# The expert layer computed densely over all 16,384 experts, 256 tokens at a time, in place of gathering each token's 128 experts

## The chip, the cores and the metric

The kernel runs on one NeuronCore of a Trainium2 chip. The metric is the device time of one launch in microseconds (us), lower is better. All data are 32-bit floats.

## What is computed

One decoder layer for a prompt of 1024 tokens and for a sample group of 8 tokens, with D_MODEL = 1024. The layer projects the normalised input (1024 to 2816 columns), runs eight 64-wide heads of a recurrent delta-rule mixer beside a causal gated MLP in chunks of 128 tokens, projects back, then applies the expert layer (PEER), a gated per-layer embedding and a final norm. The part that the change rewrites is this:

```python
def peer_ffn(h, wq, subkeys, U, V):           # U, V: (16384, 1024)
    q  = (xt @ wq).reshape(T, 8, 2, 128)
    sc = einsum('thcd,cnd->thcn', q, subkeys)  # two scores of 128 keys for each of 8 heads
    sv, si = top_k(sc, 16)                     # 16 of 128, twice
    cand = sv[:, :, 0, :, None] + sv[:, :, 1, None, :]
    cv, ci = top_k(cand.reshape(T, 8, 256), 16)
    eidx = (si0 * 128 + si1)[ci]               # 8 x 16 = 128 experts of each token
    gate = softmax(cv)
    act  = gelu(einsum('tkd,td->tk', U[eidx], x)) * gate
    out  = einsum('tk,tkd->td', act, V[eidx])
```

So each token needs 128 rows of U and 128 rows of V out of 16,384. The outputs are the final rows of both groups, the new recurrent states, the shifted rows and the normalised rows of the sample group.

## The kernel before

The prompt is worked in NB = 8 blocks of 128 tokens, the partitions of a tile; the sample group is a ninth, narrow block. Three things run beside each other in iteration i, each engine (TensorE, VectorE, ScalarE, GpSimd, and SyncE for DMA) with its own program in an order written out by hand:

- the *front* of block i: norm, 11 weight chunks `win` (each 1024 x 256, two halves of 512 KB into the two buffers `wbuf`), shift, the mixer (`half(i, 0)` and `half(i, 1)`, four heads each), 4 chunks `wout`, norm, 8 query chunks `q`, top-16 searches (`top16`), the digit stages that turn candidate numbers into expert numbers, softmax;
- the *peer* work of block i-1: 128 steps. Step k of GpSimd gathers, by an indirect DMA, one U row and one V row for each of the 128 tokens (`uring`, `vring`, 8 slots each). VectorE multiplies the U rows with the tokens and sums (`expert`, L1611), ScalarE takes gelu of four at a time, VectorE weights them (`weigh`, L1592). The weighted sum of V rows is shared: of 128 steps 74 go to TensorE as a matmul with a diagonal matrix (ScalarE builds it, `diagonals`; `sum_v`, L979), the others to VectorE (L1604);
- the *tail* of block i-2: sum, norm, per-layer embedding (L957), 4 `gate` chunks, final norm, store.

`BOTH_STAGES` and `STAGE_WEIGHTS` spread the stages of front and tail over the 128 steps. `stream` (L755) is the matmul of a weight chunk: 8 matmuls of 128 x 128 weights by 256 columns, and after them TensorE waits for its own last result before it frees the buffer. Each 32-bit matmul stands as two records in the trace, so a chunk is 16 records; a transpose is one record. `load_w` issues a chunk's two DMAs from SyncE's queue when the buffer's last reader is done. Six PSUM banks rotate among the stages, two (`acc`) hold the expert sums.

Of the kernel before, what the change touches and what calls it, by code (L numbers as in the profile page):

```python
# [6 lines left out]
F32 = mybir.dt.float32  # L28
# [6 lines left out]
P = 128  # L35
# [15 lines left out]
NU, NV = 8, 8  # L51
NI = 4
UNIT = 4
UNITS = HK // UNIT
SPREAD = 123

PE_SHARE = {0: 2, 3: 1, 9: 3, 13: 2, 26: 4}
MOST_PE = max(PE_SHARE.values())
# [15 lines left out]
PER_BLOCK = {who: sum(len(who(n)) for n in range(UNITS)) for who in (pe_experts, ve_experts)}


def summed(who, i, n, j=UNIT - 1):

    if n < 0:
        i, n = i - 1, n + UNITS  # L80
    return (i - 1) * PER_BLOCK[who] + sum(len(who(m)) for m in range(n)) + sum(e <= j for e in who(n))

TAIL_STAGES = ["t_sum", "t_norm", "t_turn", "t_xT"] + [f"gate{c}" for c in range(5)] + ["y_norm", "y"]
NORM = lambda name: [f"{name}_{part}" for part in ("mean", "var", "root", "scale")]
HALF_STAGES = lambda g: (
    [f"h{g}_{part}" for part in ("turn", "products", "TT", "TI")]
    + [f"h{g}_{part}{m}" for m in range(1, LEVELS) for part in ("merge", "update")]
    + [f"h{g}_{part}" for part in ("solve", "SR0", "dS0", "SR1", "dS1", "Y")]  # L90
)
FRONT_STAGES = (
    ["norm", "turn", "xT"] + [f"win{c}" for c in range(11)] + ["shift0", "shift1", "shift2", "lora"] + NORM("ln") + ["lora_add", "kk", "gmlp", "key", "bonus", "kk_norm", "cum", "hats0", "hats1", "masked_v"]
    + [stage for both in zip(HALF_STAGES(0), HALF_STAGES(1)) for stage in both]
    + NORM("gn") + ["gn_bonus", "gn_gate"] + [f"wout{c}" for c in range(5)] + ["norm2", "xn2", "x2T"]
    + [stage for h in range(H + 2) for stage in [f"q{h}"] + ([f"ctop{h - 2}"] if h > 1 else []) + [f"top{h}"]] + ["soft"]
    + [f"digit{half}{part}" for half in range(2) for part in "abc"] + ["expert"]
)


HALF = lambda g: {
    3 * g: [f"aT{g}", f"rT{g}", f"MakT{g}"] + [f"TXt{g}{m}" for m in range(1, LEVELS)] + [f"SR{g}0", f"dS{g}1"],
    3 * g + 1: [f"bT{g}", f"MT{g}", f"MrbT{g}"] + [f"TX{g}{m}" for m in range(1, LEVELS - 1)] + [f"U1{g}", f"dS{g}0", f"Y{g}"],
    3 * g + 2: [f"kT{g}", f"M{g}", f"X{g}1", f"X{g}2", f"MrkT{g}", f"X{g}3", f"X{g}4", f"U0{g}", f"X{g}5", f"WT{g}", f"SR{g}1"],
}
SETUP_USES = {0: ["s_sk"], 1: ["s_ws0"], 2: ["s_ws1"], 3: ["s_vec"], 4: [], 5: []}
TAIL_USES = {
    0: ["t_xT0", "gate0", "gate2"], 1: ["t_xT1", "gate1", "gate3"], 2: ["ple0"], 3: ["ple1"], 4: ["t_pT"], 5: [],
}
_IN = {b: [f"xT{b}"] + [f"win{c}" for c in range(11) if c % 2 == b] for b in (0, 1)}  # L110
# [20 lines left out]
STAGE_WEIGHTS = {
    "t_sum": 33, "t_norm": 25, "t_turn": 15, "t_xT": 13, "gate4": 10, "gate": 48, "y_norm": 10, "y": 14, "norm": 12, "norm2": 12,
    "turn": 15, "xT": 14, "win": 55, "ln_mean": 26, "ln_var": 20, "ln_root": 5, "ln_scale": 30, "shift": 32, "lora": 55,
    "lora_add": 22, "kk": 34, "gmlp": 36, "key": 26, "bonus": 38, "kk_norm": 30, "cum": 18, "hats": 26, "masked_v": 28,
    "h_turn": 42, "h_products": 32, "h_TT": 38, "h_TI": 42, "h_merge": 48, "h_update": 18, "h_update5": 8, "h_solve": 28,
    "h_SR": 14, "h_dS": 14, "h_Y": 14, "gn_mean": 20, "gn_var": 16, "gn_root": 5, "gn_scale": 24, "gn_bonus": 18, "gn_gate": 20,
    "wout4": 8, "wout": 50, "xn2": 16, "x2T": 18, "q": 40, "top": 18, "q8": 22, "q9": 20, "top9": 1, "ctop": 24, "soft": 14,
    "digita": 48, "digitb": 46, "digitc": 38, "expert": 20,  # L140
}


# [1523 lines left out]
```

## Time and profile before

| | |
|---|---|
| median of 3 runs | 4841.38 us (4822.09 to 4863.28) |
| span of the profiled execution | 4840.4 us |
| TensorE busy (matmuls) | 3142.8 us, 65% |
| VectorE busy | 3066.2 us, 63% |
| GpSimd busy | 2461.0 us, 51% |
| ScalarE busy | 867.2 us, 18% |
| moved by DMA | 1407.59 MB, 291 GB/s |
| mean granted TensorE clock | 0.809 of full |

The profiled execution has no time of its own beside its span; the span differs from the median of the runs by 1 us, so a sum over the trace can stand for the time. Busy shares are means over the whole span: a front, the peer steps and a tail overlap in it.

### The profile page before, as it was taken

The page shows a single profiled execution, that of the slowest core. Times are in us where ns is not written, and L with a number is a line of the kernel's source. Part 1 is how long each engine was busy: PE and PEld are TensorE (multiplying, and loading weights), DVE is VectorE, ACT ScalarE, POOL GpSimd, SP SyncE. Part 2 cuts the span into 40 slices and gives each one's busy share as a digit, 9 for nine tenths or more (in the row PEclk, how much of TensorE's full clock was granted, in tenths as well). Part 3 has the DMA queues.
Part 4 walks back from the last instruction along what each step waited for, and adds up shares of the span by engine and source line. Part 5 has one row for each costly group of instructions (what it writes and reads, how often), then busy time and mean ns, then how long its engine had stood idle before and what let it go on. Part 6 is the DMA issues. An engine that isn't in the chain of part 4 may idle for free.

```text
span 4840.4 us, 48177 instructions
## 1 busy us (share of the span) xinstructions
PE 3142.8 (65%) x12962; PEld 2018.9 (42%) x12962; DVE 3066.2 (63%) x6057; ACT 867.2 (18%) x1858; POOL 2461.0 (51%) x2366
## 2 busy tenths in 40 slices
PE   4744676747766487747776396747777386764486
PEld 3643454425534265324544264334544255321152
DVE  1462968539584587639594586638685385857682
ACT  1110211202112211202112111202112121121112
POOL 1013765537455564537555474537655374557551
PEclk8777798869788698878888698878889697886668
DMA  4057899968989699968999699887989689999896
GB/s 144 30 153 263 292 349 330 331 230 313 320 310 359 215 350 342 320 239 313 316 320 368 209 324 332 307 290 269 357 303 342 225 318 319 317 358 312 311 318 214
DMA packets 648503, 1407.59 MB, mean 291 GB/s; under 512 B 44137, under 2 KB 369033, under 8 KB 648210
## 3 DMA queue, kind: packets, MB, share of 16 engines
q0 software_dynamic: 297216, 1082.26, 62.0%
q1 hardware_dynamic: 350994, 321.95, 20.7%
q8 instruction: 120, 1.97, 0.2%
q14 instruction: 173, 1.42, 0.1%
HBM read 1386.84 MB, written 9.93 MB: 289 GB/s over the span
## 4 chain that ended last, share of the span: by engine, by line
PE 33%; DVE 26%; DMA 22%; issue 10%; ACT 3%; SPq 3%; POOL 2%; DVEq 0%; POOLq 0%; ACTq 0%; PEldq 0%
PE peer_acc L979 11%; DMA wbuf<-in_w_in_dram 10%; PE bank L755 9%; DVE uring L1611 4%; DMA pa<-in_norm_ffn_g_dram 3%; DVE accv L1604 3%; DMA wbuf<-in_ple_gate_w_dram 3%; DMA proj_s<-pa 3%; DMA wbuf<-in_w_out_dram 2%; PE bank L843 2%; PE bank L893 2%; PE bank L877 1%; DVE feat L1443 1%; SPq L509 1%; PE bank L891 1%
## 5 line engine op out<-in xcount | busy, mean ns | idle before, releaser
L683 POOL DMA_INDIRECT vring<-in_peer_v_dram,idx_c x1024 | 1159.1, 1132 | 1278.2 <-PE peer_acc L979 858.0
L979 PE MATMUL peer_acc<-vring,dg 128*128 128x512 f32 x2368 | 1298.6, 692 | 456.7 <-ACT dg L1023 421.0
L673 POOL DMA_INDIRECT uring<-in_peer_u_dram,idx_c x1024 | 1160.8, 1134 | 660.1 <-issue 221.2
L1611 DVE CUSTOM_DVE_ANT_0 uring<-uring,px 128x1024 f32<-128x1024 f32 x1024 | 1243.7, 1223 | 94.0 <-DMA uring<-in_peer_u_dram,idx_c 66.6
L755 PE MATMUL bank<-wbuf,xT 128*128 128x256 f32 (+1 forms) x2736 | 760.2, 436 | 593.8 <-DMA wbuf<-in_w_in_dram 489.0
L979 PEld LDWEIGHTS peer_acc<-vring,dg 128*128 128x128 f32 x2368 | 486.3, 219 | 1055.3 <-issue 742.4
L755 PEld LDWEIGHTS bank<-wbuf,xT 128*128 128x128 f32 (+1 forms) x2736 | 549.9, 206 | 826.9 <-DMA wbuf<-in_w_in_dram 535.5
L1604 DVE SCALAR_TENSOR_TENSOR accv<-vring,pact,accv 128x1024 f32<-128x1024 f32 x424 | 544.5, 1284 | 15.7 <-issue 4.8
L1592 DVE TENSOR_TENSOR pact<-pg,pgate 128x4 f32<-128x4 f32 x256 | 40.4, 158 | 706.2 <-ACT pg L1023 705.7
L843 PEld LDWEIGHTS bank<-xT,wbuf 128*128 128x128 f32 x2304 | 307.4, 215 | 55.0 <-issue 49.0
L843 PE MATMUL bank<-xT,wbuf 128*128 128x128 f32 (+1 forms) x2304 | 306.3, 294 | 13.6 <-ACT xT L1023 7.3
L1023 ACT ACTIVATE dg<-ident,pact 128x128 f32<-128x128 f32 x592 | 200.3, 392 | 528.1 <-DVE pact L1592 524.1
L665 POOL COPY idx_c<-eidx 128x4 uint32 (+1 forms) x256 | 111.2, 435 | 342.7 <-DVEq L1222 327.3
L1023 ACT ACT_TABLE_LOAD x200 | 256.6, 1283 | 21.6 <-DMA z<-in_x_prompt_dram 15.8
L723 PE MATMUL bank<-ident,z 128*128 128x128 f32 (+1 forms) x288 | 53.1, 344 | 311.5 <-DVE z L1388 132.5
L1023 ACT ACTIVATE pg<-ph 128x4 f32<-128x4 f32 x257 | 52.3, 203 | 972.9 <-DVE ph L1611 955.2
L723 PEld LDWEIGHTS bank<-ident,z 128*128 128x128 f32 (+1 forms) x288 | 43.2, 185 | 335.7 <-issue 335.7
L1023 ACT ACTIVATE uv<-bank 128x256 f32<-128x256 f32 (+4 forms) x70 | 33.2, 484 | 632.0 <-PE bank L755 575.7
L1023 ACT ACTIVATE feat<-bank 128x256 f32<-128x256 f32 (+2 forms) x133 | 55.9, 421 | 268.5 <-PE bank L755 148.7
L1441 DVE MAX8 sv<-feat 128x8 f32<-128x128 f32 (+1 forms) x144 | 41.8, 290 | 95.4 <-ACT feat L1023 87.1
L1023 ACT ACTIVATE pa<-bank 128x256 f32<-128x256 f32 (+1 forms) x63 | 24.1, 383 | 435.3 <-PE bank L755 435.3
L1381 DVE TENSOR_TENSOR x<-bank,x 128x256 f32<-128x256 f32 (+1 forms) x36 | 15.2, 423 | 131.6 <-PE bank L755 101.6
(278 smaller groups left out, 3294.7 us busy)
## 6 DMA issues: line engine op xcount, KB each, us to landing
wbuf<-in_w_in_dram SPq DMA_DIRECT2D x198, 512.0 KB, 12.3
wbuf<-in_peer_wq_dram SPq DMA_DIRECT2D x144, 512.0 KB, 10.4
wbuf<-in_w_out_dram SPq DMA_DIRECT2D x72, 512.0 KB, 9.1
wbuf<-in_ple_gate_w_dram SPq DMA_DIRECT2D x72, 512.0 KB, 10.7
uring<-in_peer_u_dram,idx_c POOLq DMA_INDIRECT x1024, 6.5
vring<-in_peer_v_dram,idx_c POOLq DMA_INDIRECT x1024, 6.4
wbuf<-in_ple_w_dram SPq DMA_DIRECT2D x18, 512.0 KB, 6.8
feat<-in_shift_mu_dram SPq DMA_DIRECT2D x9, 896.0 KB, 11.6
```

What stands on the lines that cost most here:

```text
L509: sp.dma_start(at(i + 1), pa[P - 1:P, :]).then_inc(sig("proj_stored"), 16)
L665: gp.tensor_copy(idx_c[:, n % NI, :], src).then_inc(sig("idx_copied"), 1)
L673: gp.indirect_dma_start(uring[:, s, :], None, peer_u, bass.IndirectOffsetOnAxis(ap=idx_c[:, n % NI, j:j + 1], axis=0)).then_inc(sig(f"u{s} ...
L683: gp.indirect_dma_start(vring[:, s, :], None, peer_v, bass.IndirectOffsetOnAxis(ap=idx_c[:, n % NI, j:j + 1], axis=0)).then_inc(sig(f"v{s} ...
L723: return nc.tensor.transpose(out, in_, ident[0:n, 0:n])
L755: last = mm(b[0:n, 0:WC], xT[:, k, 0:n], w[:, k, :], start=(k == 0), stop=(k == KT - 1))
L843: last = mm(b[:, c * P:c * P + n], w[:, c, k, :], xT[:, k, 0:n], start=(k == 0), stop=(k == KT - 1))
L893: heads4(i, f"TXt{g}{m}", lambda b, h, hh: mm(hd(b, h), hd(XXg, h), hd(TTg, h), start=True, stop=True), g)
L979: last = mm(acc[c][:, :], dg[:, n % 2, at, :], vring[:, s, c * 512:(c + 1) * 512], start=(n + at == 0), stop=(n == UNITS - 1 and j == pe_e ...
L1023: return nc.scalar.activation(out, in_, f, **kw)
L1604: ins = stt(accv[:, :], vring[:, s, :], act_j, accv[:, :], ALU.mult, ALU.add)
L1611: v.tensor_tensor_reduce(out=uring[:, s, :], in0=uring[:, s, :], in1=px[:, :], scale=1.0, scalar=0.0, op0=ALU.mult, op1=ALU.add, accum_out ...
```

## The change

The gathers go away. The program has one order for all engines, `PLAN`, made by `merge` from lists of stages and their weights; each engine walks through it.

1. *Fold* (once, beside the fronts of blocks 0 and 1): U is read in 128 blocks of 128 experts, each block is transposed by TensorE (8 transposes), copied out of PSUM half by ScalarE and half by VectorE, and stored to DRAM as `utT`.
2. *Gate matrix* (`gd`, for each prompt block): the expert numbers and gates are transposed; for each token a one-hot matrix of its first digit times gate and one of its second digit are multiplied (128 x 128 by 128 columns, summed over the 128 choices). VectorE makes the one-hots, TensorE makes four tokens per step in 32 steps, ScalarE copies to `staging`, SyncE stores to DRAM.
3. *Dense* (for each of 4 groups of 256 tokens, beside the fronts of the next two blocks and a tail of two blocks): for each of 128 expert blocks e, stage `U{e}`: 8 matmuls with 256 columns give 128 experts x 256 tokens; ScalarE takes gelu of two blocks at a time; stage `M{u}`: VectorE multiplies with the gate matrix, read back from DRAM; stage `V{e}`, two pairs later: 4 matmuls with 512 columns add to four accumulators. U-transposed and V blocks (512 KB each) stream through 4 slots each, in whole rows.
4. Four PSUM banks are accumulators, one holds the hidden values, three rotate for the stages (six before). The tail works on two blocks. The sample group keeps gathered rows (8 U and 8 V gathers). Sigmoids become tanh with scale 0.5.

The order is: pair 0 beside the fold; pairs 1 to 3 beside dense groups 0 to 2; the sample block and the tail of pair 2 beside dense group 3; the tail of pair 3 alone.

```diff
-NU, NV = 8, 8
-PE_SHARE = {0: 2, 3: 1, 9: 3, 13: 2, 26: 4}
+GROUPS = NB // 2
+EB = NK
+UNITS = EB // 2
+NUR, NVR = 4, 4
+NA, LAG = 3, 2
+GC, NGD = 8, 2
+RING = 3
+GD_STEPS = 32
...
+def dense_stages(g):
+    out = []
+    for u in range(UNITS + LAG):
+        mine = [f"U{2 * u}", f"U{2 * u + 1}"] if u < UNITS else []
+        if u >= LAG:
+            mine.append(f"V{2 * (u - LAG)}")
+        if u < UNITS:
+            mine.append(f"M{u}")
+        if u >= LAG:
+            mine.append(f"V{2 * (u - LAG) + 1}")
+        out += [(("dense", g), name) for name in mine]
+    return out
...
+    out = of(("setup", 0), ["setup"]) + merge(pair(0), of(("fold", 0), [f"T{e}" for e in range(EB)])) + of(("ready", 0), ["ready"])
+    for p in range(1, GROUPS):
+        out += merge((tail(p - 2) if p > 1 else []) + pair(p), dense_stages(p - 1)) + of(("ready", p), ["ready"])
...
+    return out + merge(tail(GROUPS - 2) + sample, dense_stages(GROUPS - 1)) + tail(GROUPS)
...
 @block.gpsimd
-            def gather_u(i, n, j):
-                gp.indirect_dma_start(uring[:, s, :], None, peer_u, bass.IndirectOffsetOnAxis(ap=idx_c[:, n % NI, j:j + 1], axis=0)).then_inc(sig(f"u{s}_full"), 16)
+            def load_u(c):
+                gp.dma_start(uring[:, c % NUR, :], utT[c % EB]).then_inc(sig(f"u{c % NUR}_loaded"), 16)
+            def load_v(c):
+                e = c % EB
+                gp.dma_start(vring[:, c % NVR, :], peer_v[e * P:(e + 1) * P, :]).then_inc(sig(f"v{c % NVR}_loaded"), 16)
...
 @block.tensor
+            def fold(_):
+                for e in range(EB):
+                    yield f"T{e}"
+                    pe.wait_ge(sig(f"nat{e % NVR}_loaded"), 16 * (e // NVR) + 16)
+                    wait_pos(pe, sig("fold_a"), e - 1)
+                    for k in range(4):
+                        last = turn(acc[2 * (e % 2)][:, k * P:(k + 1) * P], vring[:, e % NVR, k * P:(k + 1) * P])
...
+            def dense(g):
+                            yield f"U{e}"
+                            pe.wait_ge(sig(f"u{c % NUR}_loaded"), 16 * (c // NUR) + 16)
+                            if e % 2 == 0:
+                                wait_pos(pe, sig("gelu_done"), c // 2)
+                            for k in range(KT):
+                                last = mm(hid[:, (e % 2) * 256:(e % 2) * 256 + 256].rearrange("p (b t) -> p b t", b=2), uring[:, c % NUR, k * P:(k + 1) * P],
+                                          xg[g % 2][:, :, k, :], start=(k == 0), stop=(k == KT - 1))
...
+                            yield f"V{e}"
+                            pe.wait_ge(sig("a_ready"), c // 2 + 1)
+                            pe.wait_ge(sig(f"v{c % NVR}_loaded"), 16 * (c // NVR) + 16)
+                            for b in range(2):
+                                for half in range(2):
+                                    last = mm(acc[2 * b + half][:, :], hg[:, (c // 2) % NA, at + b * P:at + (b + 1) * P], vring[:, c % NVR, half * 512:(half + 1) * 512],
+                                              start=(e == 0), stop=(e == EB - 1))
...
+            def gd(i):
+                for q in range(GD_STEPS):
+                    yield f"gd{q}"
+                    pe.wait_ge(sig("oneh_ready"), i * GD_STEPS + q + 1)
+                    b = take(pe, me, f"gd{q}")
+                    for t in range(4):
+                        last = mm(b[:, t * P:(t + 1) * P], oneR[:, q % 2, t, :], oneL[:, q % 2, t, :], start=True, stop=True)
...
 @block.scalar
+            def dense(g):
+                    act.wait_ge(sig("u_done"), 2 * c + 2)
+                    wait_pos(act, sig("v_done"), 2 * (c - NA + 1))
+                    fn(hg[:, c % NA, :], hid[:, :], ACT.Gelu).then_inc(sig("gelu_done"), 1)
...
 @block.vector
+            def dense(g):
+                    ve.wait_ge(sig("gelu_done"), c + 1)
+                    ve.wait_ge(sig(f"gdr{k % NGD}_loaded"), 16 * (k // NGD) + 16)
+                    tt(hidden, hidden, weight, ALU.mult).then_inc(sig("a_ready"), 1)
+            def gd(i):
+                    tt(oneR[:, q % 2], bc(iota[:, :], [P, 4, NK], 1), bc(eT[:, 1, 4 * q:4 * q + 4], [P, 4, NK], 2), ALU.is_equal)
+                    for t in range(4 * q, 4 * q + 4):
+                        ins = v.tensor_scalar(oneL[:, q % 2, t % 4, :], iota[:, :], eT[:, 0, t:t + 1], eT[:, 2, t:t + 1], ALU.is_equal, ALU.mult)
-                v.tensor_tensor_reduce(out=uring[:, s, :], in0=uring[:, s, :], in1=px[:, :], scale=1.0, scalar=0.0,
-                    ins = stt(accv[:, :], vring[:, s, :], act_j, accv[:, :], ALU.mult, ALU.add)
```

## Rows read from the trace of the kernel before

**Rows 1.** The page: busy time; then 40 slices; then the chain that ended last.

```profile
PE 3142.8 (65%) x12962; PEld 2018.9 (42%) x12962; DVE 3066.2 (63%) x6057; ACT 867.2 (18%) x1858; POOL 2461.0 (51%) x2366
...
DMA  4057899968989699968999699887989689999896
...
PE 33%; DVE 26%; DMA 22%; issue 10%; ACT 3%; SPq 3%; POOL 2%; DVEq 0%; POOLq 0%; ACTq 0%; PEldq 0%
```

**Rows 2.** The page's costliest groups: busy us, mean ns | idle before, releaser.

```profile
L683 POOL DMA_INDIRECT vring<-in_peer_v_dram,idx_c x1024 | 1159.1, 1132 | 1278.2 <-PE peer_acc L979 858.0
L979 PE MATMUL peer_acc<-vring,dg 128*128 128x512 f32 x2368 | 1298.6, 692 | 456.7 <-ACT dg L1023 421.0
...
L1611 DVE CUSTOM_DVE_ANT_0 uring<-uring,px 128x1024 f32<-128x1024 f32 x1024 | 1243.7, 1223 | 94.0 <-DMA uring<-in_peer_u_dram,idx_c 66.6
L755 PE MATMUL bank<-wbuf,xT 128*128 128x256 f32 (+1 forms) x2736 | 760.2, 436 | 593.8 <-DMA wbuf<-in_w_in_dram 489.0
```

**Rows 3.** Timeline of PE, first front: start, us, operation, records, idle before.

```profile
25.45 6.21 PE L755 MATMUL bank<-wbuf,xT 128*128 128x256 f32 x16 [0.83 <-DVE xT L1283]
31.96 3.69 PE L755 MATMUL bank<-wbuf,xT 128*128 128x256 f32 x16 [0.30 <-PE bank L755]
...
100.72 6.14 PE L755 MATMUL bank<-wbuf,xT 128*128 128x256 f32 x16 [36.96 <-DMA wbuf<-in_w_in_dram]
...
119.19 3.52 PE L804 MATMUL bank<-uv,wsT 128*128 128x64 f32 x16
...
263.04 5.26 PE L843 MATMUL bank<-xT,wbuf 128*128 128x128 f32 x32 [0.73 <-ACT xT L1023]
268.60 3.81 PE L843 MATMUL bank<-xT,wbuf 128*128 128x128 f32 x32 [0.30 <-PE bank L843]
```

**Rows 4.** Timeline of PE at the end: the longest unbroken stretch of L979.

```profile
4722.12 17.43 PE L979 MATMUL peer_acc<-vring,dg 128*128 128x512 f32 x40
```

**Rows 5.** Timeline of PE amid a front: matmuls and transposes of 128 columns.

```profile
2036.61 1.06 PE L723 MATMUL bank<-ident,z 128*128 128x128 f32 x8 [2.18 <-ACT z L1023]
...
2265.43 1.05 PE L891 MATMUL bank<-ms 128*128 128x128 f32 x8
```

**Rows 6.** Windows: length, busy of PE, PEld, DVE, ACT, POOL; clock, DMA share, GB/s.

```profile
263.00:303.00 40.00, 35.73 (x288) 34.28 (x288) 26.41 (x117) 7.43 (x17) 0.00 (x0) 0.96 0.72 206
...
2783.00:2903.00 120.00, 109.92 (x649) 80.67 (x647) 98.09 (x161) 22.35 (x54) 87.12 (x85) 0.95 0.90 323
2883.00:2893.00 10.00, 10.00 (x48) 7.69 (x47) 5.20 (x11) 1.17 (x4) 5.48 (x7) 0.55 0.97 358
4739.00:4790.00 51.00, 27.80 (x93) 16.84 (x92) 16.43 (x31) 11.95 (x19) 9.20 (x8) 0.83 0.70 259
```

**Rows 7.** Groups by form: sample's sum, VectorE's peer work, operations on 128 x 512.

```profile
L1002 PE MATMUL peer_acc<-vring,sdg 128*8 128x512 f32 x32 | 13.9, 592 | 0.3 <-PE bank L755 0.3
...
L1604 DVE SCALAR_TENSOR_TENSOR accv<-vring,pact,accv 128x1024 f32<-128x1024 f32 x424 | 544.5, 1284 | 15.7 <-issue 4.8 <-DMA vring<-in_peer_v_dram,idx_c 3.8 <-DVE pact L1592 2.3
L1611 DVE DVE_READ_ACCUMULATOR2_ANT ph<- 128x1 f32 x1024 | 82.8, 81 | 0.0
L1592 DVE TENSOR_TENSOR pact<-pg,pgate 128x4 f32<-128x4 f32 x256 | 40.4, 158 | 706.2 <-ACT pg L1023 705.7
...
L1506 DVE TENSOR_TENSOR ms<-bank,ms 128x512 f32<-128x512 f32 x40 | 27.2, 680 | 1.7 <-PE bank L893 1.7
...
L1023 ACT ACTIVATE ms<-bank 128x512 f32<-128x512 f32 x40 | 23.9, 597 | 111.6 <-PE bank L891 111.3
```

**Rows 8.** Timeline of DVE, digit stages of the first front.

```profile
325.89 0.23 DVE L1420 CAST e<-hi 128x128 f32<-128x128 uint32 x1
...
333.61 0.23 DVE L1419 TENSOR_SCALAR hi<-ci 128x128 uint32<-128x128 uint32 x1
333.87 0.23 DVE L1420 CAST e<-hi 128x128 f32<-128x128 uint32 x1
...
341.59 0.29 DVE L1429 SCALAR_TENSOR_TENSOR e<-e 128x128 f32<-128x128 f32 x1
```

**Rows 9.** Timeline of POOL: the first copy of expert numbers.

```profile
343.42 0.18 POOL L665 COPY idx_c<-eidx 128x4 uint32<-128x4 uint32 x1 [327.33 <-DVEq L1222]
```

**Rows 10.** DMA issues: count, KB each, median us from issue to landing.

```profile
wbuf<-in_w_in_dram SPq DMA_DIRECT2D x198, 512.0 KB, 12.3
...
uring<-in_peer_u_dram,idx_c POOLq DMA_INDIRECT x1024, 6.5
```

More of the change, by code:

```diff
@@ L77, in summed @@
[L77 to L85, printed above, removed]
+GROUPS = NB // 2
[5 more added lines that the diff above has]
+RING = 3
+TG = 16
+GD_STEPS = 32
+SAMPLE = NB
 NORM = lambda name: [f"{name}_{part}" for part in ("mean", "var", "root", "scale")]
@@ L87 @@
 HALF_STAGES = lambda g: (
-    [f"h{g}_{part}" for part in ("turn", "products", "TT", "TI")]
-    + [f"h{g}_{part}{m}" for m in range(1, LEVELS) for part in ("merge", "update")]
+    [f"h{g}_{part}" for part in ("turnA", "turnB", "MT", "M")]
+    + [f"h{g}_{part}{m}" for m in range(1, LEVELS) for part in ("X", "T")]
     + [f"h{g}_{part}" for part in ("solve", "SR0", "dS0", "SR1", "dS1", "Y")]
 )
[L92 to L98, printed above, removed]
@@ new lines, in _ @@
+            load_params()
+            hold(sig("zero_row"), 1)
+            sp.dma_start(proj_s[0:1, :], xm[0:1, :]).then_inc(sig("zero_stored"), 16)
+            for key, name in drive(front=front, tail=tail, gd=gd, ready=ready, dense=dense, final=final, peer=peer):
+                chunk = weight_of(key, name)
+                if chunk:
+                    n = CHUNK_AT[key, chunk] + 2
+                    if n < len(CHUNKS) and CHUNKS[n][1] not in LATE:
+                        load_w(sp, n)
@@ L716, in _ @@
+            for _ in drive(fold=fold, ready=ready, dense=dense, peer=peer):
+                pass
         @block.tensor
         def _(pe):
-            eng_name[id(pe)] = "pe"
             mm = nc.tensor.matmul
@@ new lines, in final @@
+            def final(_):
+                yield "wkv"
+                pe.wait_ge(sig("ST0_ready"), NB * 2 + 1)
+                pe.wait_ge(sig("ST1_ready"), NB * 2 + 1)
+                b = take(pe, ("final", 0), "wkv")
+                for h in range(H):
+                    last = turn(b[0:64, h * HD:(h + 1) * HD], ST[:, h, :])
+                filled(("final", 0), "wkv", last)
+            for _ in drive(setup=setup, fold=fold, dense=dense, gd=gd, front=front, tail=tail, peer=peer, final=final):
+                pass
@@ L1205, in _ @@
+            for _ in drive(fold=fold, dense=dense, gd=gd, front=front, tail=tail, peer=peer, final=final):
+                pass
         @block.vector
         def _(ve):
-            eng_name[id(ve)] = "ve"
             steps = [0]
@@ L1642 @@
+            for _ in drive(setup=setup, fold=fold, dense=dense, gd=gd, front=front, tail=tail, peer=peer):
+                pass
 _INS = ['x_prompt', 'x_sample', 'state_wkv', 'state_shift', 'p_prompt', 'p_sample', 'norm_mix_g', 'w_in', 'shift_mu', 'rwkv_w0',
```

1634 lines of the change are left out of this document (860 added, 774 removed).

## The prediction

> **What bounds the kernel now.** First the busy times and the chain: TensorE 65%, VectorE 63%, GpSimd 51%, and the chain that ended last is split TensorE 33%, VectorE 26%, DMA 22% [rows 1]. No engine is full; the DMA slices stand at 8 or 9 tenths. Then the costliest groups, to see what the peer work is: 1159 us of V gathers, about as much of U gathers, 1244 us of VectorE dot products, 1299 us of TensorE's diagonal matmuls [rows 2]. The peer steps set the pace on several engines at once, and the weight chunks wait 489 us for DMAs beside them. The change takes nearly all of this away and puts matmuls in its place, so the question is what TensorE costs. For that I read its timeline, not its means: the page's mean of 436 ns for a 256-column record holds overlap and both clocks.
>
> **Unit costs of TensorE.** A chunk of 8 matmuls, 128 x 128 weights by 256 columns, takes 3.69 us in 16 records when the engine has been busy, 6.21 us after a wait [rows 3]: the two levels of the clock. A stage `U{e}` is exactly this shape. Some 0.18 us of the 3.69 is the drain that the next group overlaps; I take 3.5. `V{e}` is 4 matmuls by 512 columns, 8 records, the shape of L979: 40 records in an unbroken run took 17.43 us, 0.436 each [rows 4], so 3.45. One expert block costs 6.95 us. Bounds: 7.3 if each group pays its drain, 6.85 if a U block runs at the rate of the 512-column row.
>
> **Added on TensorE.** Dense: 4 groups x 128 blocks x 6.95 = 3558 us (3507 to 3740). Gate matrix: 8 blocks x 32 steps x 4 matmuls of 128 columns; 8 such records take 1.05 us [rows 5], so 256 x 1.05 = 269 us. Fold: 128 blocks x 8 transposes, 8 take 1.06 us [rows 5], 137 us. In sum 3964 us.
>
> **Removed from TensorE.** L979, 1299 us of its 3142.8 [rows 1, 2], and the sample's 14 us [rows 7]. The rest, fronts and tails, is 1830 us, but partly at the low clock: the 2736 records of L755 took 760 us, and at 3.5 per 16 they take 598. Corrected for that line alone the rest is 1668 us; the other lines I leave as measured. The new tail and front do the same matmuls.
>
> **So TensorE must be busy for 1668 + 3964 = 5632 us, at the high clock, with no gap.** That is 791 us more than the whole kernel takes now. Everything else is about how much idle time comes on top.
>
> **What lies where.** Of a prompt front I count 172 us of TensorE: 1668 less nine tails of 20 us (4 chunks and the per-layer part) and 105 us for the sample, by eight.
>
> *Phase 0, pair 0 beside the fold.* Here TensorE has only 2 x 172 + 2 x 34 + 137 = 549 us of work and the chain of the front decides. The first front of before, alone, handed over its experts after 343 us [rows 9]. It contains the 37 us wait for the weights behind the parameter loads [rows 3], which stays. Its parts by the timeline: up to the first query chunk 263 [rows 3], queries and searches 62, to 325, digits 18 [rows 3, 8]. Pair 0: 263, then queries with the chunks of front 1 75, digits 18, then 32 gate steps on VectorE, each one 128 x 512 operation (0.68) and four of 128 x 128 (0.26 with the spacing) [rows 7, 8], 1.7 us, 55 us and 20 us of shift and norm beside them; the rest of front 1, from the gated MLP's matmuls at 119 to the first query chunk at 263 [rows 3], 142, queries 62, digits 18, gate steps 55. Sum 708 us. The fold's 128 stages stand between these on three engines that keep one order (1.06 on TensorE, 0.6 on ScalarE, 0.7 on VectorE). Bounds 0 and 250 us; I take half, 120. Phase 0: 830 us (740 to 960).
>
> *Phases 1 to 4, dense beside fronts.* TensorE's work is 5632 - 549 - 40 (last tail) = 5043 us. On top: TensorE waits 0.30 us for its own result after each chunk [rows 3]; some 180 chunks, 54 us. Between phases the gate matrix must land in DRAM and be read back before the first `M`, and a 512 KB load takes 12.3 us to land [rows 10]; some 14 us are covered by the first four `U`, so 50 us for four starts (20 to 100). The clock falls in the mixer's narrow matmuls although the engine is never idle, 0.55 for 10.0 us busy of 10 us [rows 6]; these stay. I take 8 us for each front there, 60 us (0 to 150). Gaps where a front's stage waits for ScalarE or VectorE: about two in three stages have a dense block of 3.5 us ahead of them in the order, against 0.6 to 2 us of copying and masking. The best stretch of before, with gathers' matmuls as filler, has TensorE busy 109.92 of 120 us [rows 6]. Fuller cover, and long stretches of nothing but chunks and dense blocks: 3%, 150 us (50 to 450). Sum 5357 us.
>
> *Last tail, alone, on two blocks.* One tail of before takes 51 us from its transposes to its last norm, 13 of them for weights [rows 6]; two members together with sum and store, 80 us (60 to 110).
>
> Sum: 830 + 5357 + 80 = 6267. The span of before agrees with the median to 1 us, so nothing is added: **6260 us**, a ratio of 1.29.
>
> **What hides the rest.** VectorE loses 1244 + 545 + 83 + 40 us [rows 2, 7] and gains 256 gate steps x 1.7 = 435, 256 `M` x 0.68 = 174, 128 copies x 0.7 = 90: about 1850 us, a third of the span. ScalarE stays near 1000. The price of this is nothing so long as TensorE has a queue of dense blocks; `M{u}` waits for gelu, which waits for `U{2u+1}`, and everything behind `M{u}` on VectorE waits with it, but its reader `V` comes two pairs (14 us) later. DMA: U-transposed and V four times 134 MB, fold 134, gate matrix 134, weights 240, small loads 30, near 1075 MB in place of 1408, in whole rows; 170 GB/s against 291. A slot of the ring has three blocks, at least 21 us, to be refilled; the row nearest is 12.3 us [rows 10]. SyncE holds the gate stores and the weight chunks in one queue; at two chunks ahead it has at least 14 us per chunk. If that cover were gone a chunk would wait some 5 us, 180 x 5 = 900 us; I see no sign of it at half the present load.
>
> **Rivals.** (a) *Lockstep*: all engines keep one order with three rotating banks, so that a front's chain, not the sum of the matmuls, sets the pace, and TensorE is busy for 85% in phases 1 to 4: 830 + 5043 / 0.85 + 80 = 6840 us. For it: the stages `X`, `T` of the mixer stand with one dense block between two at most. Against: 109.92 of 120 [rows 6] with poorer filler. 0.14. (b) *The clock doesn't hold* through 5 ms of dense work and averages 0.9 there: 830 + 5357 / 0.9 + 80 = 6860. The mean over busy stretches is 0.95 and 0.96 [rows 6], falling only by waits and narrow matmuls. 0.06. (c) *Faster than before*: long unbroken streams of full matmuls run faster than the short ones of before, since weight loads and matmuls then overlap wholly. The point is where TensorE's 5632 plus some 550 us of idle time falls under 4841: a block then costs (4841 - 550 - 2074) / 512 = 4.3 us, not 6.95. Against it: 40 records unbroken took 0.436 each [rows 4] and 16 records 0.23 each [rows 3], hardly below the short runs. If an expert block took 4.0 us, the sum would be 6260 - 512 x 2.95 = 4750 us. 0.02.
>
> The Trainium skill, "TensorE: Matmul & The Clock Gate", section "Back-to-back issue gap", has a rule that speaks for (c): a sustained stream of weight loads and 512-column matmuls runs at about 131 ns per matmul, while an isolated one has 216. By it the 32-bit record, twice the isolated figure here, would sustain 0.26 us and not 0.436; estimated from that page a `V{e}` would take 2.1 us and the kernel would be faster. By [rows 4] the trace doesn't agree: its longest stream shows the isolated rate, doubled.
>
> (d) *Phase 0 and gaps cheaper than I think*: fold wholly hidden and 50 us of gaps, 740 + 5200 + 60 = 6000. It is part of the forecast's range. (e) *The change doesn't do what it says*: no; the gathers of the prompt are gone from the program, and the counts are in the loops.
>
> **How the numbers follow.** Forecast 6260, within 5980 to 6520, 0.78; (a) 0.14, (b) 0.06, (c) 0.02. The range 5970 to 6700 leaves out (c), most of (b) and the upper half of (a), and below it lies only what TensorE's floor of 5632 plus some 320 us of unavoidable idle time in phase 0 and the last tail forbids. Within 1% is about what a measurement of this kernel can tell from no change: faster 0.02, same 0.01, slower 0.97.
>
> **What would show each step.** Right: a matmul group of about 4096 U matmuls (8192 records) at 0.22 us and 2048 V matmuls (4096 records) at 0.43; TensorE above 5500 us busy, near 90% of the span, clock 0.9 or more in phases 1 to 4; the first `U` near 830 us; the four dense phases 1300 to 1420 us for three and 1100 for the last. Wrong: a U block under 3 us; TensorE idle above 10% with VectorE or DMA as releaser (a); a clock below 0.9 in stretches without a gap (b); phase 0 over 960 us.

## The result: 6224 us, 1.285 times the time before

The changed kernel takes 6223.8 us (median of 4 runs, 6219.8 to 6240.9); the kernel before takes 4843.6 us in the same runs (4822.1 to 4863.3). The ratio is 1.2849, 95% interval 1.2805 to 1.2893. The prediction was 6260 us. The profiled execution has a span of 6239.1 us.

The page of the changed kernel: busy time, the clock and DMA slices, the chain that ended last, and the costliest groups, as in [rows 1, 2].

```profile
PE 5659.9 (91%) x25978; PEld 4127.7 (66%) x25978; DVE 1998.0 (32%) x4939; ACT 1005.0 (16%) x1546; POOL 705.1 (11%) x1342
...
PEclk8887888999999999999999999999999999999999
DMA  6785864356545554456545555356545656565553
...
PE 77%; DMA 7%; DVE 5%; issue 2%; ACT 1%; SPq 0%; POOL 0%; DVEq 0%; ACTq 0%; PEldq 0%
...
L826 PE MATMUL peer_acc<-vring,hg 128*128 128x512 f32 x4096 | 1859.4, 601 | 29.5 <-PE bank L862 23.5
L809 PE MATMUL peer_hid<-xg,uring 128*128 128x256 f32 x8192 | 1847.3, 381 | 13.4 <-PE bank L862 5.5
...
L862 PE MATMUL bank<-wbuf,xg 128*128 128x256 f32 (+1 forms) x2736 | 637.8, 388 | 147.4 <-DMA wbuf<-in_w_in_dram 141.3
...
L843 PE MATMUL bank<-oneL,oneR 128*128 128x128 f32 x2048 | 296.8, 300 | 126.5 <-DVE oneL L1379 126.3
...
L761 PE MATMUL peer_acc<-ident,vring 128*128 128x128 f32 x1024 | 156.7, 305 | 64.0 <-DMA vring<-in_peer_u_dram 28.5
```

The kernel went from several engines that share the pace (TensorE 65%, VectorE 63%, GpSimd 51%) to one that is full. VectorE fell from 3066 to 1998 us and GpSimd from 2461 to 705, and both gains lie beside TensorE, which rose from 3143 to 5660, above the whole time of the kernel before. The two dense lines are 3707 us of it. They wait for almost nothing (29.5 and 13.4 us); of TensorE's 579 us of idle time, 331 stand ahead of the weight chunks (141), the gate matrix (126) and the fold (64). The clock row shows 8 and dips to 7 in the first seven slices, and 9 from there on.

Windows of the changed kernel, cut at the first `U` of each phase, after the last `V` and at the end: length, busy of PE, PEld, DVE, ACT, POOL, then clock, DMA share, GB/s.

```profile
0.00:902.00 902.00, 606.73 (x3865) 538.46 (x3865) 467.87 (x1159) 231.22 (x367) 152.72 (x310) 0.82 0.69 237
902.00:2237.60 1335.60, 1275.88 (x5900) 932.02 (x5901) 426.81 (x1090) 206.31 (x312) 135.28 (x257) 0.98 0.54 171
2237.60:3644.30 1406.70, 1327.19 (x6066) 969.35 (x6065) 438.90 (x1113) 223.68 (x336) 135.09 (x257) 0.97 0.52 166
3644.30:5053.80 1409.50, 1331.71 (x6067) 972.70 (x6067) 439.16 (x1114) 223.81 (x336) 135.17 (x257) 0.97 0.53 165
5053.80:6174.80 1121.00, 1078.12 (x3923) 685.43 (x3922) 211.71 (x444) 104.91 (x174) 146.80 (x265) 0.97 0.58 181
6174.80:6239.10 64.30, 40.30 (x165) 29.76 (x163) 13.59 (x24) 15.09 (x23) 0.00 (x0) 0.87 0.19 65
```

So TensorE is busy for 5013 of 5273 us in phases 1 to 4, 95%, and for 67% of phase 0. Phase 1 is the shortest of the three full ones; it has no tail beside it.

Timeline of TensorE in the changed kernel (start, us, records, idle before): the dense blocks in pairs, and a weight chunk that came late.

```profile
1027.86 6.74 PE L862 MATMUL bank<-wbuf,xg 128*128 128x256 f32 x16 [31.67 <-DMA wbuf<-in_w_in_dram]
...
1042.33 7.14 PE L809 MATMUL peer_hid<-xg,uring 128*128 128x256 f32 x32 [0.30 <-PE bank L862]
1049.31 7.03 PE L826 MATMUL peer_acc<-vring,hg 128*128 128x512 f32 x16
1056.18 3.62 PE L809 MATMUL peer_hid<-xg,uring 128*128 128x256 f32 x16
```

From start to start, two `U` blocks take 6.98 us and two `V` blocks 6.87: 6.93 us for a block of each, where 6.95 was forecast. The first row is what I had not forecast: TensorE idle for 31.7 us in the middle of phase 1, because in its fixed order the next thing was a weight chunk that had not landed. The dense stages behind that chunk then ran without a wait for their own loads.

### The profile page after: what moved, and what is told of

It is laid out like the page before. It is cut to its first block, busy times and chain, and to the rows that moved or that the text cites. A ratio compares the mean times of both kernels' runs of the same rounds, so it can differ in the third digit from the quotient of the medians.

```text
span 6239.1 us, 64322 instructions
## 1 busy us (share of the span) xinstructions
PE 5659.9 (91%) x25978; PEld 4127.7 (66%) x25978; DVE 1998.0 (32%) x4939; ACT 1005.0 (16%) x1546; POOL 705.1 (11%) x1342
## 4 chain that ended last, share of the span: by engine, by line
PE 77%; DMA 7%; DVE 5%; issue 2%; ACT 1%; SPq 0%; POOL 0%; DVEq 0%; ACTq 0%; PEldq 0%
PE peer_hid L809 26%; PE peer_acc L826 26%; PE bank L862 8%; PE bank L972 4%; PE bank L843 3%; PE bank L947 3%; DMA proj_s<-pa 2%; DMA xm<-proj_s 2%; DMA wbuf<-in_w_in_dram 1%; DVE oneL L1379 1%; PE bank L761 1%; DVE oneR L1377 1%; PE peer_acc L761 1%; PE bank L1061 1%; PE bank L957 1%
## 5 line engine op out<-in xcount | busy, mean ns | idle before, releaser
L826 PE MATMUL peer_acc<-vring,hg 128*128 128x512 f32 x4096 | 1859.4, 601 | 29.5 <-PE bank L862 23.5
L809 PE MATMUL peer_hid<-xg,uring 128*128 128x256 f32 x8192 | 1847.3, 381 | 13.4 <-PE bank L862 5.5
L809 PEld LDWEIGHTS peer_hid<-xg,uring 128*128 128x128 f32 x8192 | 1543.6, 191 | 304.9 <-issue 107.9
L826 PEld LDWEIGHTS peer_acc<-vring,hg 128*128 128x128 f32 x4096 | 764.5, 192 | 867.8 <-issue 854.7
L862 PE MATMUL bank<-wbuf,xg 128*128 128x256 f32 (+1 forms) x2736 | 637.8, 388 | 147.4 <-DMA wbuf<-in_w_in_dram 141.3
L862 PEld LDWEIGHTS bank<-wbuf,xg 128*128 128x128 f32 (+1 forms) x2736 | 497.0, 184 | 287.0 <-issue 180.4
L843 PE MATMUL bank<-oneL,oneR 128*128 128x128 f32 x2048 | 296.8, 300 | 126.5 <-DVE oneL L1379 126.3
L843 PEld LDWEIGHTS bank<-oneL,oneR 128*128 128x128 f32 x2048 | 279.2, 211 | 176.0 <-DVE oneL L1379 148.0
L947 PE MATMUL bank<-xg,wbuf 128*128 128x128 f32 (+1 forms) x2304 | 279.7, 279 | 11.4 <-DMA wbuf<-in_peer_wq_dram 8.1
L1379 DVE TENSOR_SCALAR oneL<-iota,eT 128x128 f32<-128x128 f32 x1024 | 283.8, 340 | 0.0
L1159 ACT ACTIVATE ms<-bank 128x512 f32<-128x512 f32 x128 | 130.6, 1051 | 251.7 <-PE bank L843 251.7
L1159 ACT ACTIVATE feat<-bank 128x512 f32<-128x512 f32 x128 | 130.4, 1051 | 235.0 <-PE bank L843 234.7
```

Source lines behind the costliest of these rows:

```text
L809: last = mm(hid[:, (e % 2) * 256:(e % 2) * 256 + 256].rearrange("p (b t) -> p b t", b=2), uring[:, c % NUR, k * P:(k + 1) * P], xg[g % 2][ ...
L826: last = mm(acc[2 * b + half][:, :], hg[:, (c // 2) % NA, at + b * P:at + (b + 1) * P], vring[:, c % NVR, half * 512:(half + 1) * 512], st ...
L843: last = mm(b[:, t * P:(t + 1) * P], oneR[:, q % 2, t, :], oneL[:, q % 2, t, :], start=True, stop=True)
L862: last = mm(b[0:n, m * WC:(m + 1) * WC], xT[:, k, 0:n], w[:, k, :], start=(k == 0), stop=(k == KT - 1))
L947: last = mm(b[:, c * P:c * P + n], w[:, c, k, :], xT[:, k, 0:n], start=(k == 0), stop=(k == KT - 1))
L1159: has_read(me, f"gd{q}", fn(staging[s % 2][:, :, 4 * (q % 4):4 * (q % 4) + 4].rearrange("p i t -> p t i"), b[:, :].rearrange("p (t i) -> p ...
```

## The experiments

Four questions: is a dense block worth its TensorE time on the path (e1, e6, e7)? What is the time of everything else, the frame (e2)? What holds up the weight chunks (e3, e4)? What does phase 0 consist of (e5)? The last two kernels follow from the answers.

**e1, half of each dot product of U.**

```diff
-                            for k in range(KT):
+                            for k in range(KT // 2):
```

> Each U stage keeps 4 of its 8 contraction steps (half of each dot product is left out). Theory, TensorE is the bound in phases 1 to 4: the time falls by what leaves TensorE, 512 blocks x 8 records x 0.218 us = 893 us, from 6224 to about 5330, less some 30 us that open as gaps. Rival, lockstep (the fronts' chain paces the phases): TensorE's busy time falls by 893 us but the span by less than 450 us, and the rest shows as TensorE idle behind ScalarE or VectorE.

Measured: 5444.1 us (5443.0 to 5445.2), ratio 1.1237 (1.1198 to 1.1277), TensorE busy 4764.7 us. TensorE lost 895 us of work and the kernel 780, 87% of it, some 80 us less than I expected; the lockstep rival (under 450) is out. The rest came back as idle time of TensorE, 679 us where it was 579: the wait for `oneL` went from 126 to 172 us, that for the `w_in` chunks from 141 to 164. TensorE's matmuls are the path, and the cover that they give to the other engines shrinks with them.

**e2, the frame without the dense matmuls.** Every stage, load, wait and count stays; `U` keeps one of its 8 matmuls, and from the third block on `V` has one of 64 columns.

```diff
-                            for k in range(KT):
+                            for k in range(1):
...
+                            if e < 2:
...
+                            else:
+                                last = mm(acc[3][:, 0:64], hg[:, (c // 2) % NA, at:at + P], vring[:, c % NVR, 0:64], start=(e == 2), stop=(e == EB - 1))
```

> Each U stage keeps 1 of 8 contraction steps, and each V stage after the first two keeps one matmul of 64 columns in place of four of 512 (nearly all dense products are left out; loads, gelu, gate multiply and all waits stay). TensorE would be busy about 1954 + 512 x 0.44 + 512 x 0.25 = 2300 us. It shows how long phases 1 to 4 last when TensorE doesn't bind. Theory: phase 0 keeps its 902 us, each of phases 1 to 3 shrinks from 1410 to 650 to 850 us (the chain of two fronts, or the 134 MB of blocks and the gate matrix at up to 350 GB/s, 530 us), phase 4 to 500 to 700, the span to 3500 to 4300. Lockstep rival: phases 1 to 3 stay above 1200 us each and the span above 5400.

Measured: 4276.7 us, one run. The windows, cut at the first `U` and before the last tail:

```profile
0.00:907.00 907.00, 614.67 (x3865) 543.31 (x3865) 468.33 (x1159) 231.27 (x366) 152.39 (x310) 0.81 0.69 236
907.00:4200.00 3293.00, 2166.72 (x11753) 1744.44 (x11753) 1503.63 (x3754) 764.87 (x1157) 551.01 (x1034) 0.79 0.80 272
```

Without nearly all of the dense matmuls, four phases still take 3293 us: 849, 894 and 898 for the three full ones against my 650 to 850, and 653 for the last. The span is within my range and the lockstep rival is out again. TensorE was busy for 2824 us, not for 2300. I had taken the summed records of the two dense lines (3707 us) out of the busy time, but those records overlap, and at a granted clock of 0.79 the other lines take longer (`oneL` times `oneR` 358 us, 297 in the changed kernel). So with next to no expert arithmetic this design is only 12% below the kernel before. It isn't a floor, as e7 shows. The longest waits of TensorE in that run (us in total, times, longest):

```profile
PE bank L846 <- DVE oneL L1382: 272.6, 173, 33.1
PE bank L865 <- DMA wbuf<-in_w_in_dram: 248.2, 42, 46.9
PE peer_acc L830 <- DVE hg L1368: 108.4, 8, 28.8
```

**What delays the chunks.** In phases 1 to 4 of the changed kernel TensorE waits four times for `w_in` chunks, 93.5 us in all: the 31.7 us above, 29.0 in phase 2, 29.5 in phase 3, and 3.3 once. The first three each stand behind one copy, described below; there are six such copies in these phases, and the other three leave no such gap. One more, in phase 0, has a gap of 41.5 us behind it. SyncE's own timeline and the DMA view of the one in phase 2 (the DMA view has 40 slices of 1.5 us: busy tenths, then GB/s):

```profile
2396.08 0.68 SPq L497 DMA_DIRECT2D xm<-pa  x1
2396.81 20.53 SPq L498 DMA_DIRECT2D proj_s<-pa  x1
2417.39 0.76 SPq L503 DMA_DIRECT2D xm<-proj_s  x1
2418.25 0.42 SPq L511 DMA_DIRECT2D feat<-in_shift_mu_dram  x1
2418.72 24.20 SPq L405 DMA_DIRECT2D wbuf<-in_w_in_dram  x4
...
DMA  7078980931007336000799920000067000189998
GB/s 289 36 177 311 283 282 34 242 129 35 23 25 231 150 112 266 27 23 27 132 396 382 336 88 27 24 29 24 29 128 239 27 29 24 35 217 366 293 327 212
```

Line 497 shifts the projected rows down by one token, 127 partitions of 7 KB from SBUF to SBUF, 889 KB. While it moves, the core's DMA rate drops again and again to 23 to 29 GB/s, with the busy share of the 16 engines at 0 tenths. The next chunks were issued behind it in the same queue. The kernel before has the same copy; its DMA view from 413 to 455 us, when front 1 reaches it, is plainer still, 13 slices of 1.05 us in a row at 21 to 36 GB/s. The last row is a window inside them (its last three numbers are clock, DMA share and GB/s):

```profile
DMA  9999999999999999998999993000000000000048
GB/s 384 401 400 393 396 399 389 395 398 389 376 439 426 395 418 399 396 365 318 376 365 309 361 357 127 36 21 32 21 28 25 28 28 21 25 28 28 25 65 272
...
439.00:452.00 13.00, 0.00 (x0) 0.00 (x0) 0.00 (x0) 0.00 (x0) 0.00 (x0) 0.50 0.07 27
```

A share of 0.07 is about one engine of 16, and 889 KB at 27 GB/s take some 34 us.

The Trainium skill, "DMA: Bandwidth & Descriptors", section "Why a DMA increments its semaphore by 16 and not by 1", has the rule behind it: the number of engines is the largest one up to 16 that divides the slowest dimension of both sides, so that 127 partitions get one engine and 112 get 16. The share of 0.07 agrees for 127 partitions; e3 and e4 test the split.

**e3, the copy split into 112 and 15 rows, in the changed kernel.**

```diff
-                    sp.dma_start(xm[1:P, :], pa[0:P - 1, :]).then_inc(sig("prev_loaded"), 16)
+                    sp.dma_start(xm[1:113, :], pa[0:112, :]).then_inc(sig("prev_loaded"), 16)
+                    sp.dma_start(xm[113:P, :], pa[112:P - 1, :]).then_inc(sig("prev_loaded"), 16)
...
-                ve.wait_ge(sig("prev_loaded"), 32 * i + (32 if prompt else 16))
+                ve.wait_ge(sig("prev_loaded"), 48 * i + (48 if prompt else 16))
```

> The copy of 127 rows of the projection, shifted by one partition (889 KB from SyncE), is issued as 112 and 15 rows; the rest is the changed kernel as it is. Theory: in the trace of the changed kernel the DMAs run at 21 to 29 GB/s for some 30 us after this copy, the rate of one engine of 16, and everything queued behind it on that engine waits, the weight chunk for TensorE too (31 us idle three times, 41 us once). With the rows spread the copy lands in some 5 us: 80 to 120 us less, about 6120. Rival, the waits come from SyncE's order (the stores and their holds ahead of the weight chunks), not from the spread: under 20 us change.

Measured: 6049.8 us (6040.3 to 6055.6), ratio 1.2489 (1.2458 to 1.252), 174 us below the changed kernel, more than I expected. The order of SyncE is the same, so the rival is out. TensorE's wait for `w_in` chunks is 23.9 us in all (141.3 before the split) and 9.7 at the longest. Its wait for `oneL` fell too, from 126.3 to 93.3, and its own busy time from 5659.9 to 5627.4, with the mean granted clock at 0.967 where it was 0.951. In the profiled executions, which are 201 us apart, phase 0 gives 57 us (the first `U` comes at 844.9 us and not at 902.0) and the later phases the rest. SyncE's timeline at a copy:

```profile
2301.73 0.91 SPq L498 DMA_DIRECT2D xm<-pa  x1
2302.68 1.82 SPq L499 DMA_DIRECT2D proj_s<-pa  x1
2304.56 0.44 SPq L504 DMA_DIRECT2D xm<-proj_s  x1
2305.11 0.37 SPq L512 DMA_DIRECT2D feat<-in_shift_mu_dram  x1
2306.21 13.09 SPq L405 DMA_DIRECT2D wbuf<-in_w_in_dram  x4
```

The one-row store behind the copy (line 499 here, 498 above) issues in 1.8 us where it sat for 20.5, and the four chunk loads behind it in 13.1 and not in 24.2.

**e4, the same edit in the kernel before.**

> The same edit in the kernel before. There the chain holds 28 to 38 us of this store and copy for most of the 8 blocks, and 22 to 28 us of weight loads behind it. Theory: 8 blocks x 20 to 30 us come off the chain, but the expert steps beside them set part of the pace: 60 to 200 us less, about 4700. Rival: these stretches are hidden behind the expert steps of the block before and only move the idle time: within 20 us of 4843.

Measured: 4542.1 us (4526.7 to 4553.6), ratio 0.9372 (0.9344 to 0.94). This is 308 us less than the kernel before in the same runs (4850.4), above my range; the rival (within 20 us) is out. TensorE's waits in it, with the `w_in` chunks at 205.8 where they were 489.0 in the kernel before; the wait for the diagonal matrices is as it was (421.0 before):

```profile
PE peer_acc L980 <- ACT dg L1024: 416.6, 103, 17.3
PE bank L756 <- DMA wbuf<-in_w_in_dram: 205.8, 83, 11.2
```

So more than half of the wait that I had read in [rows 2] as contention with the gathers was one copy on one engine. The 37 us wait of the first front in [rows 3] was this copy too. It comes right behind the copy, and in this run, at the same chunk, it is 6.9 us:

```profile
70.98 5.40 PE L756 MATMUL bank<-wbuf,xT 128*128 128x256 f32 x16 [6.85 <-DMA wbuf<-in_w_in_dram]
```

The edit is worth almost twice as much here, where no engine is full, as in the changed kernel. There only four of eight copies leave a long gap in TensorE; behind the other four it has other stages to do.

**e5, no fold.** U is read as it stands and not transposed first.

```diff
-    out = of(("setup", 0), ["setup"]) + merge(pair(0), of(("fold", 0), [f"T{e}" for e in range(EB)])) + of(("ready", 0), ["ready"])
+    out = of(("setup", 0), ["setup"]) + pair(0) + of(("ready", 0), ["ready"])
...
-                gp.dma_start(uring[:, c % NUR, :], utT[c % EB]).then_inc(sig(f"u{c % NUR}_loaded"), 16)
+                gp.dma_start(uring[:, c % NUR, :], peer_u[(c % EB) * P:(c % EB + 1) * P, :]).then_inc(sig(f"u{c % NUR}_loaded"), 16)
```

> Left out: the 1024 fold matmuls with their VectorE evictions and stores; the U blocks are loaded as they stand, so the U that the dense stage reads is not the transposed one. The prediction priced the fold at 120 us on the path (0 to 250). In the trace of the changed kernel the fold has 156.7 us of TensorE and 64 us of idle time ahead of it, all before the first dense step at 902 us. If phase 0 ends with TensorE and the waits of the fold: the first dense step moves from 902 to 710 to 780 us and the time falls by 120 to 190 us, to 6035 to 6105. If the loads of phase 0 set its end (DMA share 0.69 there), the first dense step moves by less than 50 us and the time falls by less than 50.

Measured: 6051.0 us (6026.3 to 6056.7), ratio 1.2502 (1.2468 to 1.2536), 173 us less. The first `U` moves from 902.0 to 720.6 us. The fold is 181 us of phase 0 (in e1, e2 and e6, which keep the fold, the first `U` comes at 901 to 907 us), about its 157 us of TensorE and part of its waits: the front's chain leaves TensorE idle a third of the time there, and still hides nearly none of it. Whether TensorE's order or the fold's own traffic does that (the DMA share of phase 0 is 0.69 with it and 0.35 without) this run doesn't tell. The pair alone takes 721 us, where I had put it at 708.

**e6, no multiply by the gate matrix.** Only the instruction goes; its waits and counts stay.

```diff
-                    tt(hidden, hidden, weight, ALU.mult).then_inc(sig("a_ready"), 1)
+                    ve.sem_inc(sig("a_ready"), 1)
```

> Left out: the VectorE multiply of h by the gate matrix (1024 of 512 elements, 176.2 us busy), so the output lacks the gate factor; every wait and count stays. My theory: VectorE is beside TensorE in the dense stage, so the time falls by 0 to 25 us. Rival (the hand-over from U through VectorE to V stands on the path, once for every block of hidden units): it falls by 100 to 176 us.

Measured: 6222.1 us (6218.2 to 6242.2), ratio 1.2864 (1.2825 to 1.2903): no difference from the changed kernel's 1.2849. VectorE's 176 us of `M` cost nothing, and the two pairs between `U` and `V` cover the hand-over. Together with e1 this says that in this kernel a dense block costs TensorE's time alone.

**e7, the dense operands as 16-bit floats.** The same instructions, with the transposed U, V, the gated hidden values and the normalised rows in half the width; PSUM, gelu and all else stay 32-bit.

```diff
-        uring = sb("uring", [P, NUR, D])
+        uring = sb("uring", [P, NUR, D], F16)
+        xg16 = [sb(f"xg16_{k}", [P, 2, KT, P], F16) for k in range(2)]
...
-                                          xg[g % 2][:, :, k, :], start=(k == 0), stop=(k == KT - 1))
+                                          xg16[g % 2][:, :, k, :], start=(k == 0), stop=(k == KT - 1))
...
-                    tt(hidden, hidden, weight, ALU.mult).then_inc(sig("a_ready"), 1)
+                    hidden16 = hg16[:, c % NA, :].rearrange("p (e g t) -> p e g t", e=2, t=TG)
+                    tt(hidden16, hidden, weight, ALU.mult).then_inc(sig("a_ready"), 1)
```

> The dense stage's operands (transposed U, V, h times gate, the normalized rows) are 16-bit floats and not 32-bit ones; instructions, loops and waits are otherwise as in the changed kernel, with one more ScalarE copy for the rows and V cast in its load. My theory (the time is TensorE's 32-bit matmuls): the 3706.7 us of the two dense lines fall to about a quarter, 930 us, TensorE is busy 2850 to 2950 us, and the frame sets the time, which with nearly all dense matmuls left out took 4277: 4150 to 4500 us. Rival (a dense step is bound by its hand-overs or loads and not by the passes of TensorE): over 5200 us.

Measured: 4200.7 us (4198.0 to 4201.9), ratio 0.8676 (0.8652 to 0.8699). This is within my range, though TensorE is busy for 3126 us and not for 2850 to 2950: the two dense lines sum to 1100 us, not 930. The kernel is 2023 us shorter, with 2534 us less of TensorE. The edit also cuts what the DMAs move from 1116 to 813 MB; that TensorE and not the loads was the bound rests on e1, where the loads stayed as they were. The kernel even stands 76 us below e2, which has almost no dense matmuls. So e2 is no floor: it moves 1115 MB, and its granted clock is 0.79 where e7 has 0.87. Its weight chunks alone take 44 us more of TensorE (614 us, 570 here, for 2432 records). Which of the two weighs more was not tested. The two longest waits of TensorE are those of e2, `oneL` 252.2 us and the `w_in` chunks 170.5. The third, 81.2 us, is for the product with the gate matrix, 4.2 us in the changed kernel. The two dense lines still make up 12% of the chain that ended last, so the dense work is not wholly hidden.

**e8, 16-bit operands and the split copy.**

> The kernel with 16-bit dense operands, and the copy of 127 rows issued as 112 and 15 rows. With TensorE no longer full, the stall of the w_in loads behind that copy is not covered, as in the kernel before, where the split was worth 308 us: 3850 to 4250 us, 200 to 350 below the same kernel without the split, and below the kernel before with the split (4542). Rival (the frame is set by the one-hot matrices on VectorE and the gate matrix): within 100 us of the kernel without the split.

Measured: 3967.7 us (3961.1 to 3976.4), ratio 0.8195 (0.8174 to 0.8216), 233 us below e7 and 574 below the kernel before with the same split (e4, on another chip, where the kernel before took 4850). TensorE's timeline in it:

```profile
919.80 1.91 PE L814 MATMUL peer_hid<-xg,uring 128*128 128x256 f16 x16 [0.30 <-PE bank L867]
921.54 1.89 PE L831 MATMUL peer_acc<-vring 128*128 128x512 f16 x8
923.27 0.93 PE L814 MATMUL peer_hid<-xg,uring 128*128 128x256 f16 x7
```

From start to start two `U` blocks take 1.74 us and two `V` blocks 1.73, so a block of each is 1.74 us against 6.93: a factor of 3.98, with one record for each matmul in place of two. The Trainium skill, "FP8 and Floating Point Precision", section "TensorE Precision Notes", has 32-bit matmuls go through the array in four passes. The factor of 3.98 agrees. A 16-bit matmul of 256 columns takes 0.109 us here, 2.35 columns in a nanosecond, which is about one for each cycle at the 2.4 GHz level; a 32-bit one takes 0.436 (6.98 us for 16 of them). The long stream that my case (c) needed, faster than the short ones, shows in neither width.

**e9, the one-hot matrices in 16 bits too.**

```diff
-        oneR = sb("oneR", [P, 2, 4, P])
-        oneL = sb("oneL", [P, 2, 4, P])
+        oneR = sb("oneR", [P, 2, 4, P], F16)
+        oneL = sb("oneL", [P, 2, 4, P], F16)
+        iotah = sb("iotah", [P, NK], F16)
```

> The kernel with 16-bit dense operands and the split copy, and the one-hot matrices and gate values (oneL, oneR) in 16-bit floats as well, built from a 16-bit row of indices for oneL. In the kernel that this starts from, at 3967.7 us, the gate matmuls are busy 326.6 us and TensorE waits 152.0 us for oneL; VectorE takes 339 ns for a oneL and 683 ns for a oneR. If the gate matrix is on the path: its matmuls fall to about 110 us and the wait shrinks with VectorE's shorter instructions, so 3967 falls by 150 to 350 us, to 3620 to 3820. If it is beside the stages and their loads: the time falls by less than 80.

Measured: 3906.1 us (3898.4 to 3909.5), ratio 0.8063 (0.8045 to 0.8081), 62 us less than e8. By its size this is the second of my two cases, but the trace doesn't show the gate matrix beside the path. The first `U` comes at 800.0 us where it was at 835.5, 35 us of the 62. The gate matmuls fell from 326.6 to 133.4 us busy (I had 110). VectorE builds a `oneL` in 309 ns and not 340, hardly faster, and TensorE, done sooner, waits longer for it:

```profile
PE bank L849 <- DVE oneL L1389: 226.9, 203, 5.0
...
L1389 DVE TENSOR_SCALAR oneL<-iotah,eT x1024: 301/309/448, 392.7 to 3208.8; 128x128 f16<-128x128 f16 x171
```

The first row is from the waits (152.0 in e8), the second from the view of the tile (min, median, max in ns). TensorE waits 203 times in 256 gate steps: they are bound by VectorE's five instructions for four tokens, and a way to cut these was not tried. This is the fastest kernel of the study. What the kernel before would gain from 16-bit operands was not tried.

## Why the prediction was right, step by step

**TensorE must be busy for 5632 us: right.** 5660 measured. The expert block is 6.93 us (6.95 forecast). The gate matrix is 297 us by the page (269), the fold 157 (137); their records are counted with some overlap, as those of the dense lines are, which sum to 3707 where 512 blocks of 6.93 are 3548. The term that carried the forecast came from two unbroken runs of before [rows 3, 4] and not from the page's means; by the mean of 436 ns for L755 in [rows 2], a `U` block would have been 7.0 us, twice its cost, and the whole some 1800 us too long. One reading of [rows 3] doesn't hold for both of its rows: the chunk of 6.14 us at 100.72 us has a granted clock of 0.60, the one of 6.21 us at 25.45 has 1.00, so its length isn't shown to be the clock. Nothing in the sum hangs on it.

**Phase 0, 830 us: 902 measured, within its bounds.** The pair alone was right as a number (721 measured in e5, 708 forecast), with a wrong cause in it: "the 37 us wait for the weights behind the parameter loads" was the copy on one engine. It did stay, at 41.5 us, because the copy stayed; with the copy split it is 9.7. The fold was under-priced, 181 and not 120: halfway between bounds was no better than a guess, and the value was near TensorE's own time for it. Of the 902 us, 57 are the single-engine copy (e3).

**Phases 1 to 4, 5357 us: 5273 measured.** The three full phases and the last came as expected (1336, 1407, 1410 and 1121 us). The gaps were right in sum: 260 us idle, where I had 54 + 50 + 150. Their parts were not. TensorE waited for the first gated values once, 4.2 us and not 50, and 90 us are the three long waits behind the copy, which I had not foreseen. The 84 us too much are in TensorE's work: 5013 us measured, 5043 and 60 for the clock forecast. The granted clock was 0.97 to 0.98 and fell in the places that I named, the mixer's narrow matmuls; what that cost was not measured by itself.

**The last tail, 80 us: 64.** TensorE's 40 us in it were right. So the sum 902 + 5273 + 64 = 6239, the profiled span, has errors of +72, -84 and -16 against its forecast of 6267. That it lands within 1% is partly luck, as the errors cancel; each part alone is off by 2 to 20%.

**One sentence was wrong: "I see no sign of it" on the cover of the weight chunks.** The sign was there: waits of up to 48 us on DMA for `w_in` in the kernel before, where a load's median is 12.3 us [rows 10]. I read the 489 us of [rows 2] as contention and took it to go with the gathers. 283 us of it were the copy (e4), and 174 us of the copy's cost are in the changed kernel (e3). It did not hurt the forecast, since 37 us in phase 0 and 150 us of gaps stood there for other reasons: a right sum over a wrong cause, and luck.

**The side terms.** VectorE 1998 us (1850 forecast): a `oneL` takes 340 ns with its two per-partition scalars where I took 260 with spacing, 82 us for 1024 of them; the rest was not traced. ScalarE 1005 (1000), 1116 MB (1075). VectorE's multiplies cost nothing in the dense phases (e6); its one-hot matrices did, 44.5 us of TensorE's waits there.

**The rivals.** (a) Lockstep: refuted, 95% busy and not 85%. (b) The clock: refuted, 0.97 to 0.98 and not 0.9. (c) The faster stream: refuted, 6.93 us against 4.3; e8 shows what it takes to get under that point, a quarter of the time for each matmul. (d) A hidden fold and 50 us of gaps: refuted, 181 us and 260. (e) holds as said. The prediction gives its range twice, 5980 to 6520 and 5970 to 6700; 6224 lies in both.

## What to carry to other kernels

When a change swaps memory-bound gathers for dense matmuls, add up the busy time of the engine that gets the work first, from unbroken runs in the trace at the clock it will have; if that alone exceeds the present time, no order of the stages can save it. Here the width of the operands did (1.285 became 0.82 with 16-bit dense operands and one split copy). A wait several times as long as the median landing time of its transfer may have a cause of its own: look in the DMA view for slices at a low, flat GB/s. Before believing that an engine's gaps will hide a new stage, run the kernel without that stage: here a phase with TensorE idle a third of the time hid almost nothing of it.

## What the hardware showed beyond that

- A copy of 127 partitions from SBUF to SBUF ran at 21 to 36 GB/s, with a DMA share of 0.07, and held the loads behind it in its queue; issued as 112 and 15 partitions, eight such copies cost 308 us less in one kernel and 174 in the other.
- The granted clock averaged 0.97 to 0.98 over each of four phases, 5.27 ms of nearly continuous matmuls. It fell to 0.50 in the long waits, and also with TensorE busy without a gap, in the mixer's 64-column matmuls (the two rows below, clock third from the end). In e2, with short matmuls and gaps in place of the dense ones, it was 0.79.

```profile
2426.00:2436.00 10.00, 0.00 (x0) 0.00 (x0) 0.00 (x0) 0.00 (x0) 0.00 (x0) 0.50 0.24 73
2688.00:2702.00 14.00, 14.00 (x64) 12.21 (x64) 3.39 (x8) 0.00 (x0) 0.00 (x0) 0.50 0.32 90
```

- ScalarE's copy of a 128 x 512 tile of the gate matrix out of PSUM took 1051 ns, against 597 for gelu of a tile of the same size out of the hidden bank. The copy writes its tile in another order than it reads it; no run here tests whether that is the cause. It stayed off the path in the dense phases.

```profile
L1150 ACT ACTIVATE hg<-peer_hid 128x512 f32<-128x512 f32 x256 | 152.9, 597 | 2077.9 <-PE peer_hid L809 2077.9
...
L1159 ACT ACTIVATE ms<-bank 128x512 f32<-128x512 f32 x128 | 130.6, 1051 | 251.7 <-PE bank L843 251.7
```
